# One decoder step in fp32: a stage's first weight block ahead of the LayerNorm's statistics, and other pitches of the tiles

## What is computed

```python
def _layer(x, ...):
    x = _layernorm(DN_ALPHA * x + 0.5 * _swiglu(x, ffn1_wg, ffn1_wu, ffn1_wd), ln1_g, ln1_b)
    m, ... = _mixer(x, ...)
    x = _layernorm(DN_ALPHA * x + m, ln2_g, ln2_b)
    x = _layernorm(DN_ALPHA * x + 0.5 * _swiglu(x, ffn2_wg, ffn2_wu, ffn2_wd), ln3_g, ln3_b)

def _layernorm(x, g, b):
    mu = jnp.mean(x, axis=-1, keepdims=True)
    var = jnp.mean(jnp.square(x - mu), axis=-1, keepdims=True)
    return (x - mu) * lax.rsqrt(var + LN_EPS) * g + b

def _swiglu(x, wg, wu, wd):
    return (jax.nn.silu(x @ wg) * (x @ wu)) @ wd
```

## Time and profile before

| what | us |
|---|---|
| median of 3 runs | 1463.64 (1460.6 to 1466.78) |
| the profiled execution | 1468.18 |
| its span, first to last instruction | 1466.4 |
| PE busy | 1430.5 |
| DVE busy | 880.1 |
| ACT busy | 641.0 |

### The profile page before, as it was taken

One profiled execution on the slowest core, in us unless ns is written; L12 is line 12 of the kernel. 1 busy time (PEld: TensorE's weight loads), 2 busy tenths in 40 slices (PEclk: granted clock), 3 DMA queues, 4 the chain that ended last, 5 costly groups with the idle time before them and its releaser, 6 DMA issues.

```text
span 1466.4 us, 25592 instructions
## 1 busy us (share of the span) xinstructions
PE 1430.5 (98%) x10700; PEld 1415.1 (97%) x10700; DVE 880.1 (60%) x1128; ACT 641.0 (44%) x825; POOL 29.3 (2%) x62
## 2 busy tenths in 40 slices
PE   7999999999999999999999999999999999999996
PEld 7999999999999989999989999999999999999996
DVE  5555566587655675554675555576875557655544
ACT  4444345344334564443464443453523345544433
POOL 1000000000000000000000000000000000000000
PEclk9999999999999999999999999999998999999999
DMA  7444444545545544444444444544454544544451
GB/s 252 171 169 172 158 162 172 189 169 170 204 144 175 196 144 171 156 162 166 175 158 157 160 169 159 170 154 165 157 203 144 187 147 144 173 160 159 168 180 54
DMA packets 39564, 243.60 MB, mean 166 GB/s; under 512 B 4528, under 2 KB 4544, under 8 KB 15808
## 3 DMA queue, kind: packets, MB, share of 16 engines
q1 hardware_dynamic: 32976, 219.30, 43.1%
q0 software_dynamic: 5936, 22.01, 4.3%
q10 hardware_dynamic: 576, 1.18, 0.2%
HBM read 238.97 MB, written 3.50 MB: 165 GB/s over the span
## 4 chain that ended last, share of the span: by engine, by line
PE 92%; DVE 5%; ACT 1%; issue 1%; DMA 1%; SPq 0%; DVEq 0%
PE ps L373 27%; PE ps L374 27%; PE ps L375 27%; PE ps L554 2%; PE ps L545 2%; PE ps L412 2%; PE ps L413 1%; PE ps L417 1%; DVE wlo L880 1%; DVE y L1029 1%; DVE y L1037 1%; PE ps L560 1%; DMA raw<-in_ffn_wu 1%; DVE xl L1045 1%; ACT whi L653 1%
## 5 line engine op out<-in xcount | busy, mean ns | idle before, releaser
L880 DVE TENSOR_TENSOR wlo<-raw,whi 128x1024 fp32r<-128x1024 f32 x448 | 511.0, 1147 | 368.2 <-ACT whi L653 368.1
L653 ACT CAST whi<-raw 128x1024 fp32r<-128x1024 f32 x448 | 441.0, 987 | 569.3 <-PE ps L375 487.4
L373 PE MATMUL ps<-xh,whi 128*128 128x288 f32 x1984 | 590.0, 297 | 0.0
L374 PE MATMUL ps<-xl,whi 128*128 128x288 f32 x1984 | 586.1, 295 | 0.0
L375 PE MATMUL ps<-xh,wlo 128*128 128x288 f32 x1984 | 585.3, 295 | 0.0
L374 PEld LDWEIGHTS ps<-xl,whi 128*128 128x128 f32 x1984 | 377.3, 190 | 0.7
L373 PEld LDWEIGHTS ps<-xh,whi 128*128 128x128 f32 x1984 | 376.1, 190 | 1.1 <-issue 0.4
L375 PEld LDWEIGHTS ps<-xh,wlo 128*128 128x128 f32 x1984 | 376.8, 190 | 0.0
L373 PE MATMUL ps<-hh,whi 128*128 128x288 f32 (+1 forms) x1088 | 323.4, 297 | 0.0
L374 PE MATMUL ps<-hl,whi 128*128 128x288 f32 (+1 forms) x1088 | 319.7, 294 | 0.0
L375 PE MATMUL ps<-hh,wlo 128*128 128x288 f32 (+1 forms) x1088 | 319.5, 294 | 0.0
(11 more groups left out here) (169 smaller groups left out, 891.5 us busy)
## 6 DMA issues: line engine op xcount, KB each, us to landing
raw<-in_w_in SPq DMA_DIRECT2D x48, 1024.0 KB, 5.0
raw<-in_ffn_wu SPq DMA_DIRECT2D x44, 1024.0 KB, 4.9
raw<-in_ffn_wg SPq DMA_DIRECT2D x43, 1024.0 KB, 4.9
raw<-in_ffn_wd SPq DMA_DIRECT2D x32, 1024.0 KB, 4.9
raw<-in_ffn_wd SPq DMA_DIRECT2D x16, 768.0 KB, 4.1
pool<-in_cache_k POOLq DMA_DIRECT2D x16, 512.0 KB, 4.7
pool<-in_cache_v POOLq DMA_DIRECT2D x16, 512.0 KB, 4.6
raw<-in_w_o SPq DMA_DIRECT2D x8, 1024.0 KB, 5.0
```

The source lines that it names most:

```text
L373: mm(out, wh, mh, start=start, stop=False)
L374: mm(out, wh, ml, start=False, stop=False)
L653: s_.copy(whi[:, s, k0:k1, :], raw[:, s, k0:k1, :]).then_inc(hi_ready, 1)
L880: return v.tensor_tensor(out, full, high.bitcast(F32), sub)
```

## The change

PE takes the first block of a stage before the statistics. The LayerNorm's output is x' = (y - mean) * rstd * g + b, so W x' = rstd * (W (g*y) - mean * (W g)) + W b. The tiles g*y are made in xh and xl as soon as y is there (`gained`, `gained_pair`), two more columns hold g and b (`gains`; tile width T + 2 = 290), and the block gives W (g*y), W g and W b in one pass (`early_block`). The statistics' matmuls stand behind its first tile. Afterwards DVE computes (mean * W g - W (g*y)) * rstd into hf (`correct_first`), and ACT writes W b minus that back into the PSUM banks of the block (first_ready). Then fills, if there are any, then the second block with the normal tiles (`second_block`). The gained tiles lie where the normal ones come later, so xh 0 to 3 wait for the first half of the early block and xh 4 to 7 for the second. The 20 warming matmuls are gone. Blocks are numbered and loaded in the new order: first block, fills, second block.

The pitch of xh, xl, hh and hl goes from 288 to 320 words (1280 bytes), that of whi and wlo from 288 to 256 words.

```diff
+PITCH, SHIFT = 320, 24
-        whi = sb("whi", [P, 2, 8, T], F32R)[:, :, :, 0:BC]
-        wlo = sb("wlo", [P, 2, 8, T], F32R)[:, :, :, 0:BC]
+        whi = sb("whi", [P, 2, 8, BC], F32R)
+        wlo = sb("wlo", [P, 2, 8, BC], F32R)
+        xh_wide = sb("xh", [P, KD, PITCH], F32R)
+        xl_wide = sb("xl", [P, KD, PITCH], F32R)
+        xh, xl = xh_wide[:, :, 0:T], xl_wide[:, :, 0:T]
+        hh = sb("hh", [P, KF, PITCH], F32R)[:, :, 0:T]
+        hl = sb("hl", [P, KF, PITCH], F32R)[:, :, 0:T]
...
+            def early_block(n, q, blocks, behind_first):
+                s = n % 2
+                pe.wait_ge(drained, n - blocks)
+                for h, (k0, k1) in enumerate(halves(KD)):
+                    pe.wait_ge(lo_ready, 2 * n + h + 1)
+                    for k in range(k0, k1):
+                        pe.wait_ge(gy_ready, (KD + 1) * q + k + 2)
+                        for t in range(2):
+                            c = slice(t * P, (t + 1) * P)
+                            last = products(ps[:, t, 0:T + 2], whi[:, s, k, c], wlo[:, s, k, c],
+                                            xh_wide[:, k, 0:T + 2], xl_wide[:, k, 0:T + 2], k == 0, k == KD - 1)
+                        if k == 0:
+                            behind_first()
+                    last.then_inc(pe_half, 1)
...
+            def second_block(n, q):
+                pe.wait_ge(drained, n - 2)
+                stream(n, n % 2, KD, x_tiles, 2, ready=lambda k: pe.wait_ge(x_ready, KD * (q + 1) + k + 1))
...
-                        for _ in range(WARM):
-                            mm(ps[:, 6, 0:2 * BC], hh[:, 0, 0:P], hh[:, 0:2, 0:BC], start=True, stop=True)
...
                 def norm(n, l, ln):
...
                     for k in range(KD):
                         act.wait_ge(normed, KD * q + k + 1)
+                        if k in (0, KD // 2):
+                            act.wait_ge(pe_half, 2 * (n + 1) + 1 + k // (KD // 2))
                         shifted(xh, k).then_inc(xh_ready, 1)
+                        if k == KD // 2 - 1:
+                            act.wait_ge(pe_half, 2 * (n + 1) + 2)
+                            s_.copy(gain[:, :, :], ps[:, 0:2, T:T + 2]).then_inc(gain_ready, 1)
+                        if fills == 1 and k in (1, 4):
+                            split_later(1)
+                    split_later(2)
+                    act.wait_ge(scaled_first, q + 1)
+                    act.wait_ge(gain_ready, q + 1)
+                    for t in range(2):
+                        s_.activation(ps[:, t, 0:T], hf[:, t, :], ACT.Identity, scale=-1.0,
+                                      bias=gain[:, t, 1:2]).then_inc(first_ready, 1)
                     for k in range(KD):
                         shifted(x, k).then_inc(x_full, 1)
+                    split_later(len(later))
...
+                    def correct_first():
+                        dve.wait_ge(gain_ready, q + 1)
+                        for t in range(2):
+                            od.did(v.scalar_tensor_tensor(hf[:, t, :], mean[:, :], gain[:, t, 0:1], ps[:, t, 0:T],
+                                                          mult, sub))
+                        od.last()
+                        v.tensor_tensor(hf[:, :, :], hf[:, :, :], rstd[:, :].unsqueeze(1).to_broadcast([P, 2, T]),
+                                        mult).then_inc(scaled_first, 1)
...
+                        if more and k == 1 and not fills:
+                            lo(n + 2, 1)
+                        if more and k == 4:
+                            correct_first()
+                        if len(fills) == 1 and k in (2, 5):
+                            lo(n + 3, k // 3)
+                    for i, f in enumerate(fills):
+                        evict(*f, fill_bank(i, len(fills)))
+                        if i > 0:
+                            lo(n + 3 + i, 0)
+                            lo(n + 3 + i, 1)
```

More of the change, by code:

```diff
@@ L38, in __init__ @@
     def __init__(self, L, KF, KB):
-        self.size, self.at = [], []
+        self.size, self.at, self.fills, self.done = [], [], [], {}
         down = (8, 8, KF - 16)
+        before = ()
         for l in range(L):
             at = {}
-            for name, sizes in (("F1", [8] * KF), ("D1", down * 4), ("G0", [8] * len(FILLS[l][0])),
-                                ("Z", [8] * 12), ("B", [8, KB] * 12), ("O", [8] * 4),
-                                ("G1", [8] * len(FILLS[l][1])), ("F2", [8] * KF), ("D2", down * 4),
-                                ("G2", [8] * len(FILLS[l][2]))):
-                at[name] = len(self.size)
-                self.size += sizes
-            self.at.append(at)
-        self.done = {}
-        for l in range(L):
-            for i, name in enumerate(("G0", "G1", "G2")):
-                for j, (kind, of, _) in enumerate(FILLS[l][i]):
-                    self.done[of, kind] = self.at[l][name] + j + 1
+            gaps = {"F1": before, "Z": FILLS[l][0], "F2": FILLS[l][1]}
+            for name, sizes in (("F1", [8] * KF), ("D1", down * 4), ("Z", [8] * 12), ("B", [8, KB] * 12),
+                                ("O", [8] * 4), ("F2", [8] * KF), ("D2", down * 4)):
+                fills = gaps.get(name, ())
+                if name in gaps and (l, name) != (0, "F1"):
+                    self.fills.append([(len(self.size) + 1 + i, f) for i, f in enumerate(fills)])
+                at[name] = len(self.size) + len(fills)
+                self.size += [8] * len(fills) + list(sizes)
+            self.at.append(at)
+            before = FILLS[l][2]
+        assert not before
+        self.fills.append([])
+        for gap in self.fills:
+            for n, (kind, l, _) in gap:
+                self.done[l, kind] = n
     def fills_done(self, l, kind):
@@ L259, in fill_source, with gap, gains @@
             return I["w_k_mem" if kind == "k" else "w_v_mem"][l, c]
-        def gap(l, ln):
-            at, name = plan.at[l], ("G0", "G1", "G2")[ln]
-            return [(at[name] + i, f) for i, f in enumerate(FILLS[l][ln])]
-        splits = [3 * l + ln for l in range(L) for ln in range(3) if gap(l, ln)]
+        def gap(q):
+            return plan.fills[q]
+        def gains(l, ln):
+            r = ROWS[f"ln{ln + 1}_g"]
+            return pts[:, l, r:r + 2 * KD].rearrange("p (c k) -> p k c", c=2)
+        splits = [q for q in range(3 * L) if gap(q)]
         def fill_bank(i, count):
-            return 6 if (count - 1 - i) % 2 == 0 else 0
+            return 6 if (count - 1 - i) % 2 == 0 else 2
         @block.sync
@@ L277, in load, with fills, ffn @@
                 sp.dma_start(raw[:, s, 0:src.shape[1], :], src).then_inc(raw_full[s], 16)
+            def fills(gap):
+                for n, f in gap:
+                    load(n, n % 2, fill_source(f))
             for l in range(L):
                 at = plan.at[l]
-                def ffn(k, f0, d0):
-                    start = l == 0 and k == 1
-                    if start:
+                def ffn(k, f0, d0, gap):
+                    if l == 0 and k == 1:
                         src = I["ffn1_wg"][0, 0]
@@ L288, in ffn @@
                         sp.dma_start(raw[:, 1, :, :], I["ffn1_wu"][0, 0]).then_inc(raw_full[1], 16)
-                    with sp.Fori(1 if start else 0, PAIRS_F) as i:
+                    else:
+                        n = f0 - len(gap)
+                        load(n, n % 2, I[f"ffn{k}_wg"][l, 0])
+                        fills(gap)
+                        load(f0 + 1, (f0 + 1) % 2, I[f"ffn{k}_wu"][l, 0])
+                    with sp.Fori(1, PAIRS_F) as i:
                         for s, w in enumerate((f"ffn{k}_wg", f"ffn{k}_wu")):
@@ L491, in ffn @@
                 def ffn(f, f0, d0, ln):
-                    fills = 1 if l + f == 0 else len(gap(l - 1, 2) if f == 0 else gap(l, 1))
                     def pair(i):
@@ L732, in norm @@
                     s_.activation(sq[:, 1, :], y[:, KD - 1, :], ACT.Square).then_inc(sq_ready, 1)
-                    if fills:
-                        hi(n + 2, 1)
+                    if more:
+                        gained(l, ln, KD - 1)
                     act.wait_ge(stats_psum, 2 * q + 1)
@@ L1016, in norm @@
                         v.tensor_tensor(sums[:, kind, 0], sums[:, kind, 0], tile, add).then_inc(summed, 1)
+                    if more:
+                        gained(l, ln, KD - 2)
                     dve.wait_ge(pe_half, 2 * n + 2)
```

170 lines of the change are left out of this document (86 added, 84 removed).

## The result

| what | us |
|---|---|
| before, median of 4 runs | 1464.34 (1460.6 to 1466.78) |
| changed, median of 4 runs | 1485.06 (1483.37 to 1490.93) |
| ratio | 1.0145, 95% interval 1.0122 to 1.0168 |
| the profiled execution of the changed kernel | 1490.93 (its span 1488.8) |

A forecast was written before the change was run, and what follows sets the result against it. PE, busy 98% with back-to-back matmuls, was taken to bound the kernel. Boundary terms and extra columns gave +11.5 us at full clock, clock drops +6: +17.5 us on the 1463.64 us median, 1481 us, range 1451 to 1492.

The forecast's parts named there:

- The three waits: In front of third blocks at three boundaries: PE stands for DVE's product behind tanh, 5.0, 5.0 and 5.8 us.
- mixer of layer 0: FFN entry behind this mixer, one fill: third block's wait plus 1.7 us for sums delayed by gained tiles, +2.6 us.
- mixer of layer 1: Boundary without a fill: 0.86 us from gained tiles, third block starting at 1260.0 against 1256.46, +3.6 us.
- the sum for FFN2: Layer 0, one fill: ACT's queue from last xh tile to product, 756.05; PE goes on at 757.4, +1.4 us.
- FFN1 of layer 0: Four fills: 2.2 us waits before the fourth fill and second block, +4.4 less 0.5 for a short wait, +3.9 us.
- Forecast +6 as 3 x 2.0: Clock drops behind the three long new waits, 2.0 us each, +6 us.
- the term I had left at its lower end: Clock drops behind the two waits of 2.2 us in layer 0: priced at nothing, up to 2.7 us each otherwise.
- The two extra columns: 240 matmuls by 0.9 ns, 0.2 us: Early blocks: columns for g and b lengthen 240 matmuls by 0.9 ns each, 0.2 us in all.
- I take 131.5 ns unchanged: All matmuls: the new tile pitches leave the start-to-start distance at 131.5 ns, no cost or gain.
- My bound: Pitch effect on some 9,900 matmuls: 1 ns either way, 10 us, from means of 295 ns with xl, 294 with hl.
- Rival (3): All 9,900 matmuls: new pitch separates moving tiles from weights, 3 ns each gives 1451, 4 ns 1441; chance 0.20.
- The wait stays: Layer 0: PE's 2.6 us wait for a split behind DVE's eviction stays about as long; layer 1: 2.8 us stays.

The follow-up runs named there:

- Experiment 2: Changed kernel with ACT's eight x tiles written after the first pair in three stages that begin as an FFN: 1472.69 us.
- Experiment 9: Changed kernel with x tiles behind the first pair, first fill's eviction and third block's splits between tiles 4 and 5, gained tiles after the last residual: 1472.84 us.
- experiment 5: Kernel before with the change's tile pitches alone (320 and 256 words): 1468.41 us, ratio 1.0016.
- experiment 6: Changed kernel with whi, wlo, hh and hl back at 288 words, xh and xl at 290: 1504.21 us.
- experiment 1: Changed kernel with DVE splitting the next block before evicting the fill, behind LayerNorms with several fills: 1479.5 us.
- experiment 4: Changed kernel with 32 matmuls on old data behind the second block of three FFNs, filling the long waits: 1483.5 us.
- 12: Kernel before with the first fill's eviction and third block's splits moved earlier at the two LayerNorms with several fills: 1466.09 us, ratio 1.0006.
- The best version: Changed kernel with reordered ACT and DVE queues, x tiles behind the third block's split in layer 1's mixer too: 1455.37 us, ratio 0.9942.
- experiment 10: Changed kernel with x tiles behind the first pair or the fourth block's splits, and several splits and the first fill's eviction moved earlier: 1459.62 us, ratio 0.9965.
- experiments 7: Kernel before with SHIFT 64 for 24, putting moving tiles and weights at the same address modulo 256 bytes: 1469.75 us, ratio 1.0033.

## Why the prediction was right

**What bounds.** The mechanism was right. The third block was the place to look at, and product, tanh and the queue before them its price. The three waits were forecast at 5.0, 5.0 and 5.8 us (mixer of layer 0, FFN2 of layer 0, mixer of layer 1; for FFN2 the forecast's own times, 751.9 and 757.4, give 5.5) and came at 5.1, 5.6 and 5.8 by the distance between the starts of the matmuls around them; the two of 2.2 us before the fourth fill and the second block at 2.3 and 2.2; those in the second block behind layer 1's mixer at 1.2 and 1.7, as forecast. Experiment 2 shows that of the first three 3.3 to 3.5 us each are ACT's x tiles.

In the sum for FFN2 one term is missing, the last xh tile's own 0.43 us on ACT: the sum gives 756.05, and the 756.5 that is used came from DVE's split, which by its own terms ends at 756.04. With the tile both give 756.5. From that tile to the product the trace has 7.39 us (765.91 to 773.30), and 756.5 says 7.45.

**The terms.** From the last residual to the third block the boundaries grew by 6.2 us (FFN1 of layer 0), 1.4 (mixer of layer 0), 1.3 (FFN2 of layer 0), -1.4 (FFN1 of layer 1) and 2.5 (mixer of layer 1). In front of the mixers' boundaries PE waits longer for the sums, by 1.7 us in layer 0 (2.06 for 0.34) and 0.8 in layer 1, forecast 1.7 and 0.86:

```profile
519.91 1.84 PE L475 MATMUL ps<-pool,ones 128*128 128x288 f32 x4 [2.06 <-DVE pool L1084]
```

With them the mixer of layer 0 comes to +3.1 (forecast +2.6), FFN2 of layer 0 to +1.3 (+1.4), and the mixer of layer 1 to +3.4 (+3.6). FFN1 of layer 0 has 3.9 forecast and one more slow stretch in it: in 244.15 to 247.3 and in 254.4 to 257.6 PE ran 16 and 17 fill matmuls at 0.50, 1.3 and 1.2 us of loss, where the kernel before has the first alone. That is the term I had left at its lower end: waits of 2.2 us can lower the clock, though behind the last of them (262.09) it held. The waits there grew by 4.2 us: 4.4 as forecast for the two new ones (they came at 4.3), less 0.1 where I had taken 0.5 off for a short one. The rest, some 0.4 us, is slower spacing and the 290 columns. FFN1 of layer 1 has -0.2 forecast and -1.4 measured: the slow stretch behind its wait is 3.4 us long where it was 6.8.

**The clock.** Forecast +6 as 3 x 2.0; the three stretches cost 1.5, 2.5 and 2.2, 6.2 us. That the whole account has +7.2 hides more: the second stretch in layer 0 comes on top, the one in layer 1 is shorter, and one is new behind the mixer of layer 0, where PE has waited 2.1 us for the sums. The forecast had priced that wait and no clock behind it:

```profile
520.40:523.80 3.40, 3.40 (x14) 3.11 (x13) 1.71 (x3) 1.61 (x3) 0.00 (x0) 0.50 0.70 284
```

0.9 us of it fall ahead of the last residual (from the sums' matmuls to the residual it is 2.59 us where it was 1.68), so that this boundary is +4.0 in all. Experiment 9, in which that wait is gone, has full clock there. After the waits of 1.8 to 2.5 us that experiment 2 leaves in front of the third blocks the clock held at three places, while it fell behind waits of 2.1 and 2.2 us here: the length of the last wait alone doesn't decide it. What the Trainium skill says (TensorE: Matmul & The Clock Gate, What's actually happening), that activity releases the throttle, the run with matmuls in the waits bears out.

**What was mis-sized.** "The two extra columns: 240 matmuls by 0.9 ns, 0.2 us": a matmul of 290 columns comes 135.0 ns behind the one before (from 1256.29 to 1260.07 there are 28), at layer 0 136.6; it is 3.3 to 5 ns and about 1 us. And the step "I take 131.5 ns unchanged" gave the right number by luck. I priced the pitch as a change to the old kernel, where experiment 5 confirms nothing. What it does is to hold off 17 to 19 us that tiles of 290 words would bring (experiment 6); a change without it would have been above the range. My bound, 1 ns from xl and hl, was a comparison of two sets with the same offset, as I wrote, and so no bound; 2 ns exist. Rival (3), with a faster matmul by the Trainium skill's formula (TensorE: Matmul & The Clock Gate, Wait - 56ns, not 53.3ns?), found nothing: the lowest distance that an FFN had in any run here is 130.6 ns, not the estimate of 122.5.

**What had no place in the forecast.** "The wait stays" at FFN1 of layer 0 and of layer 1 was right in the sum, but I had named the eviction as its cause; experiment 1 shows the LayerNorm's tiles. Of the 3.3 us of slower matmuls at full clock some 1 us are the 290 columns; the rest goes with this one execution and not with the change, as far as the profiles tell: experiment 4 has the same tiles and order, and 914 matmuls in 580 to 700 us where this profile has 902.

## What to carry to other kernels

Where work is pulled ahead of a wait, follow the block behind it: the time that PE saves is worth only what the slowest queue in front of the next bank gives. Here it was eaten by eight tiles that nobody needed for another 150 us and that stood in front of tanh; moving them and a few splits turned +1.4% into -0.6%. And a wait that has gone from one block is to be looked for at the next one: two of these edits (experiments 9 and 12) only moved it. A layout that changes nothing by itself can still be needed by the edit beside it, so undo it in both kernels before calling it idle.

## What the runs showed of the hardware

**The spacing of equal matmuls has several values and keeps one through an FFN.** A stretch of 120 us in an FFN, the same code and granted clock; the first and the third kernel have the same tiles too. Before, changed, and before without the warming matmuls, in this order, each one row of the windows of its kernel:

```profile
580.00:700.00 120.00, 120.00 (x913) 120.00 (x913) 63.74 (x64) 50.55 (x58) 0.00 (x0) 1.00 0.47 160
```

```profile
580.00:700.00 120.00, 120.00 (x902) 120.00 (x901) 64.98 (x67) 51.45 (x60) 0.00 (x0) 1.00 0.46 159
```

```profile
580.00:700.00 120.00, 120.00 (x921) 120.00 (x921) 64.77 (x65) 50.89 (x57) 0.00 (x0) 1.00 0.47 160
```

913, 902 and 921 matmuls: 131.7, 133.3 and 130.6 ns from start to start. In the changed kernel the distance is 133.3 in two stretches (from 262 to 320 us and from 551 to 740), 131.7 in nearly all others; in the run without warming it is 130.6 in three of the four FFNs, and that is some 6 of the 9 us by which that profiled execution is shorter than the one before, while its median is not shorter. The best version's predecessor (experiment 10) shows 133.3 from 540 to 720 as well. Within an FFN it doesn't change, but for experiment 6; it changes at the boundaries between stages, and nothing that I saw in the code foretells it. Over a whole run 1 ns is 10 us, as much as the scatter between runs of one kernel, and it is why the value of the warm clock in experiment 4 stays open. A single profile of this kernel can't tell 5 us; two profiles are compared by gaps and by slow stretches, not by their spans.

**The place of the tiles costs without a wait.** In 40 to 160 us every profile here with the moving tiles 96 bytes behind the weights modulo 256 has 913 or 914 matmuls, 131.7 ns; the one with both at the same place has 906 (132.8), the one with tiles of 290 words 902 (133.3), and the medians are 4.5 and 17 to 19 us up (experiments 7 and 6). PE is "busy" all the time, and only the count in a window shows it. Which property of the addresses it is stays open.
